# Input projection, token-major rows, merge gates and RWKV-7 in one interleaved stage of a hybrid decoder layer

## What is computed

```python
mod = silu(c) @ w_ada + b_ada                       # sh_m, sc_m, g_m, sh_f, sc_f, g_f
h = x * (1 + sc_m) + sh_m
q_a, kvc, kvs, kvw, g_a, p_b, q_c, k_c, v_c, g_mrg = split(h @ w_in)   # 1024 x 8472
# A: compressed, selected and window attention on q_a, kvc, kvs, kvw, g_a
# B: RWKV-7 on p_b (1792 columns = r, k, v, xw, xa, xg)
prev = concat(shift_prev, p_b[:-1]);  xm = p_b + (prev - p_b) * mu
# per token: decay, a = sigmoid(..), kk = normalised k, then for each of 8 heads
S = S * d + (S @ -kk) (kk * a)^T + v k^T;   out = S @ r
o_b = (groupnorm(out) + bonus) * g
# C: dilated attention, windows (128,1), (512,4), (2048,16), on q_c, k_c, v_c and the caches
m = sum_b sigmoid(g_mrg[b]) * (o_b_branch @ w_br[b])
x = LN(alpha * x + g_m * (m @ w_o));  then a SwiGLU feed-forward and a second LN
```

## Time and profile before

| what | us |
|---|---|
| median of three timed executions | 2869.45 |
| the profiled execution, its own device time | 2877.22 |
| its span, first to last instruction | 2875.4 |
| TensorE busy | 2102.3 (73%) |
| VectorE busy | 1359.8 (47%) |
| ScalarE busy | 297.2 (10%) |
| GpSimd (POOL) busy | 494.6 (17%) |
| granted TensorE clock, mean | 0.81 of full speed |

### The profile page before, as it was taken

One profiled execution on the slowest core, in us unless ns is written; L12 is line 12 of the kernel. 1 busy time (PEld: TensorE's weight loads), 2 busy tenths in 40 slices (PEclk: granted clock), 3 DMA queues, 4 the chain that ended last, 5 costly groups with the idle time before them and its releaser, 6 DMA issues. The chain is left out here.

```text
span 2875.4 us, 36912 instructions
## 1 busy us (share of the span) xinstructions
PE 2102.3 (73%) x15746; PEld 1782.1 (62%) x15746; DVE 1359.8 (47%) x2017; ACT 297.2 (10%) x673; POOL 494.6 (17%) x502
## 2 busy tenths in 40 slices
PE   4999639931346665599994999406785994999995
PEld 2999638810236664599993666303434874999994
DVE  3233202656664444566632566263662336444344
ACT  0111001000200000000002444101211100000000
POOL 0000022110009960222101454202230000000000
PEclk7999869965567555699975698657897997999998
DMA  5433369784013990433303000124354202333220
GB/s 199 155 114 135 106 257 198 196 197 154 0 32 103 322 310 16 148 118 131 112 1 111 1 1 1 36 56 171 129 205 157 69 1 68 88 88 88 81 74 32
DMA packets 229943, 320.40 MB, mean 111 GB/s; under 512 B 91279, under 2 KB 168137, under 8 KB 224596
## 3 DMA queue, kind: packets, MB, share of 16 engines
q1 hardware_dynamic: 184994, 182.63, 20.8%
q0 software_dynamic: 24320, 79.94, 8.6%
q10 hardware_dynamic: 20466, 55.48, 5.7%
HBM read 290.15 MB, written 79.95 MB: 129 GB/s over the span
## 5 line engine op out<-in xcount | busy, mean ns | idle before, releaser
L2344 PE MATMUL sdi_acc<-hT,sdi_w 128*128 128x272 f32 x768 | 178.9, 397 | 15.6 <-DMA sdi_w<-in_w_in_dram 15.6
L1661 POOL TENSOR_SCALAR pat_s<-pat_s,pat_st 128x31 f32<-128x31 f32 (+2 forms) x144 | 127.3, 902 | 287.1 <-DVE pat_st L1689 238.7
L2344 PEld LDWEIGHTS sdi_acc<-hT,sdi_w 128*128 128x128 f32 x768 | 147.6, 192 | 46.9 <-DMA sdi_w<-in_w_in_dram 16.1
L1124 PE MATMUL cmp_pH<-cmp_RTh,cmp_w1h 128*128 128x256 f32 (+1 forms) x576 | 171.2, 297 | 4.9 <-issue 4.9
L269 PE MATMUL ffn_acc<-ffn_hh,ffn_wh 128*128 128x272 f32 x704 | 146.2, 289 | 36.2 <-DVE ffn_wl L260 36.2
L1124 PE MATMUL cmp_pH<-cmp_RTh,cmp_w1l 128*128 128x256 f32 (+1 forms) x576 | 167.8, 291 | 3.0 <-issue 3.0
L1124 PE MATMUL cmp_pH<-cmp_RTl,cmp_w1h 128*128 128x256 f32 (+1 forms) x576 | 167.9, 292 | 0.0
L269 PE MATMUL inp_acc<-inp_hh,inp_wh 128*128 128x272 f32 (+1 forms) x688 | 143.4, 290 | 17.3 <-DVE inp_wl L260 17.3
L269 PE MATMUL ffn_acc<-ffn_hh,ffn_wl 128*128 128x272 f32 x704 | 146.2, 289 | 0.0
L269 PE MATMUL ffn_acc<-ffn_hl,ffn_wh 128*128 128x272 f32 x704 | 145.6, 288 | 0.0
L269 PE MATMUL inp_acc<-inp_hl,inp_wh 128*128 128x272 f32 (+1 forms) x688 | 142.8, 289 | 0.0
(11 more groups left out here) (439 smaller groups left out, 4424.9 us busy)
## 6 DMA issues: line engine op xcount, KB each, us to landing
out_dram<-in_cache_dil_dram SPq DMA_DIRECT2D x1, 32704.0 KB, 155.0
ffn_w<-in_w_ffn_dram SPq DMA_DIRECT2D x60, 512.0 KB, 3.8
sdi_w<-in_w_ada_dram ACTq DMA_DIRECT2D x8, 2048.0 KB
inp_w<-in_w_in_dram SPq DMA_DIRECT2D x7, 2048.0 KB, 7.8
sdi_w<-in_w_in_dram ACTq DMA_DIRECT2D x6, 2048.0 KB
PT<-inp_o ACTq DMA_DIRECT2D x42, 272.0 KB, 2.1
sdi_kv<-in_cache_dil_dram POOLq DMA_DIRECT2D x36, 256.0 KB, 10.0
sdi_kv<-in_cache_dil_dram SPq DMA_DIRECT2D x36, 256.0 KB
```

The source lines that it names most:

```text
L1124: i = pe.matmul(pH[:, w % 2, 0:nw], l, r, start=(q == 0 and n == 0), stop=(q == 15 and n == 2))
L1661: pool.tensor_scalar(s[:, u % 3, b, 0:n], s[:, u % 3, b, 0:n], st[:, u % 4, 2, b:b + 1], None, ALU.mult).then_inc(sd, 1)
L2344: i = pe.matmul(acc[:, n % 2, h, 0:HN], w[:, l % NW, k, j * P:(j + 1) * P], m["hT"][:, k, h * HN:(h + 1) * HN], start=(k == 0), stop=(k == ...
```

## The change

1. `in_projection`, `token_major` and `rwkv` are replaced by one phase, `project_and_mix`, with one block. `Projection` has 67 tiles, now with the 24 gate tiles (so these too are made of three rounded products), in the order p_b, kvc, kvs, kvw, k_c, v_c, g_a, q_a, q_c, gates. A tile's weights come as one load of 512 KB; the cast to the high half is ScalarE's, the subtraction VectorE's. There is one accumulator instead of four. Token-major rows, shift rows and the g_a gates are turned on TensorE from the tile in SBUF (L409, L415), kept by ScalarE, and stored by SP, inside the next tile.
2. `Mixer` does RWKV in 128-token pieces: the 32 sample columns first, then four pieces of the prompt, through elementwise work, chunk pair, state and norm. Several copies out of PSUM (X of every level among them) move from VectorE to ScalarE.
3. Every engine's program is made of Python generators that yield the due time of their next step, in abstract units; `weave` always takes the one that is due first. A piece of the prompt takes 18 units, a projection tile 2.5, and the first 14 tiles (p_b) come before unit 0. So the order on each engine is fixed when the program is built; the waits are the semaphores' as before. The last projection tile is due at unit 132.5; the mixer's last step at about 123.
4. `conditioning` splits h (8 casts on ScalarE, then 8 subtractions on VectorE) at its end, and stores x (8 stores of 272 KB) into rows of PT that are no longer used; `merge` loads it back (8 loads, behind the branch weights and ahead of the gates).
5. `sample_dilated` has no gate tiles any more, only the 8 loads of `w_ada`; softmaxes come after its loads 1, 3 and 5. V is multiplied in its own order instead of through a transposed view. The 81 stores of new cache rows come at the end of its SP program.
6. The four cache copies move from the RWKV chunks' SP program to that of `compress`, behind its first loads.

```diff
+def weave(*programs):
+    heads = [[next(p), i, p] for i, p in enumerate(programs)]
+    while heads:
+        first = min(heads, key=lambda x: (x[0], x[1]))
+        try:
+            first[0] = next(first[2])
+        except StopIteration:
+            heads.remove(first)
...
+    NW = 3
+    ORDER = ("pb", "kvc", "kvs", "kvw", "kc", "vc", "ga", "qa", "qc", "gm")
...
+    def at(self, n, k=0.0):
+        return n - 14 if n < 14 else (n - 14 + k / KD) * PACE
...
+        for n, (c, t, rows) in enumerate(self.tiles):        # Projection.tensor
+            for k in range(KD):
+                yield self.at(n, k)
+                if k == 0:
+                    pe.wait_ge(self.low, n + 1)
+                    if n:
+                        pe.wait_ge(self.evac, n)
...
+ITER = 18
+PROLOGUE = 17
+PACE = 2.5
+def start_of(t):
+    return PROLOGUE + ITER * t
...
 # compress, SP
                 sp.dma_start(per[:, :], a["phi_pe"][0]...).then_inc(loaded, 16)
+                shift_caches(sp, a, m["copied"])
 # merge, SP
+                for k in range(KD):
+                    sp.dma_start(m["xT"][:, k, :], saved_rows(a, k)).then_inc(xl, 16)
                 for n in range(KD):
 # sample_dilated
-SOFTMAX_AFTER = [(2, 3), (5, 3), (9, 3)]
-    loads = [("w_in", c, t) for c, _, t in GROUPS if t >= TILE0["gm"]]
...
-    loads += [("w_ada", k, t) for t in (2 * KD, 4 * KD) for k in range(0, KD, 2)]
+    loads = [(k, t) for t in (2 * KD, 4 * KD) for k in range(0, KD, 2)]
...
+                new_cache_rows(sp, a, m["token_rows_out"])
...
-                    c(dve.tensor_tensor(t3, t3, s[:, g, :].unsqueeze(1).to_broadcast([P, HD, NK]), ALU.mult))
+                    c(dve.tensor_tensor(V[:, :, :], V[:, :, :], s[:, g, :].unsqueeze(2).to_broadcast([P, NK, HD]), ALU.mult))
```

More of the change, by code:

```diff
@@ L50 @@
 TILE0 = {}
+TILES = {}
 GROUPS = []
@@ L210, in _, with saved_rows @@
                 dve.wait_ge(xev, KD)
-                modulate(dve, chain, m["hT"], m["xT"], m["modT"], 0, KD)
+                modulate(dve, chain, hT, xT, m["modT"], 0, KD)
+                dve.sem_inc(modulated, 1)
+                for k in range(KD):
+                    dve.wait_ge(high, k + 1)
+                    split_low(dve, m["hl"][:, k], hT[:, k], m["hh"][:, k]).then_inc(vch, 1)
 ADA_W = 2048
+def saved_rows(a, k):
+    t = TILE0["kvc"] + k if k < TILES["kvc"] else TILE0["vc"] + k - TILES["kvc"]
+    return a["PT"][t * P:(t + 1) * P, :]
 def modulation_step(pe, out, cT, w, k):
@@ L659, with __init__ @@
     HH = HR // 2
[L661 to L670 removed]
+    def __init__(self, nc, a, m, ot, sem, sb):
+        self.a, self.out, self.ot = a, m["sample_state_out"], ot
+        self.S = sb("sS", [P, self.HR, HD])
+        self.tmp = sb("stmp", [P, self.HH, HD])[:, :, :]
+        self.qs = sb("sq_", [P, DT, 5, HD])
+        self.q = [self.qs[:, t] for t in range(DT)]
         self.vs = sb("vs", [P, DT, self.HR])
@@ L875, in _ @@
[L875 to L882 removed]
+                weave(proj.tensor(pe), mix.prepare_tensor(pe), mix.chunk_tensor(pe), mix.state_tensor(pe), mix.norm_tensor(pe))
@@ L1324, in merge @@
         acc = ps("acc", [P, 4, 2, 512])
-        mT = m["hT"]
-        loaded, wol, sig, done, used, ch, out, oused = (sem(s) for s in ("loaded", "wol", "sig", "done", "used", "ch", "out", "oused"))
+        mT = sb("mT", [P, KD, NT])
+        loaded, xl, wol, sig, done, used, ch, out, oused = (sem(s) for s in ("loaded", "xl", "wol", "sig", "done", "used", "ch", "out", "oused"))
         gl = [sem(f"g{i}") for i in range(2)]
@@ L2235, in sample_dilated @@
         wl = [sem(f"w{i}") for i in range(NW)]
-        gdone, gevac, mdone, mevac, mturned, wused = (sem(n) for n in ("gdone", "gevac", "mdone", "mevac", "mturned", "wused"))
-        gst = [sem(f"gst{i}") for i in range(2)]
+        mdone, mevac, mturned, wused = (sem(n) for n in ("mdone", "mevac", "mturned", "wused"))
         NROW = [32, 20, 20]
@@ L2419, in build @@
         with ExitStack() as mixer:
-            for name, chunks in (("hT", KD), ("oaT", 4), ("obT", 4), ("ocT", 2)):
+            m["obT"] = mixer.enter_context(nc.sbuf_tensor("obT", [P, 4, NT], F32))
+            with ExitStack() as first:
+                for name in ("hh", "hl"):
+                    m[name] = first.enter_context(nc.sbuf_tensor(name, [P, KD, NT], F32R))
+                for phase in FIRST:
+                    phase(nc, a, m)
+            for name, chunks in (("oaT", 4), ("ocT", 2)):
                 m[name] = mixer.enter_context(nc.sbuf_tensor(name, [P, chunks, NT], F32))
-            for phase in BEFORE_NSA:
-                phase(nc, a, m)
+            sample_dilated(nc, a, m)
             with ExitStack() as nsa:
+                m["hT"] = nsa.enter_context(nc.sbuf_tensor("hT", [P, KD, NT], F32))
                 m["kcT"] = nsa.enter_context(nc.sbuf_tensor("kcT", [P, DB + 1, 256], F32))
@@ L2443, in _ @@
             sp.wait_ge(m["copied"], 16 * 4)
-BEFORE_NSA = [conditioning, in_projection, token_major, sample_dilated, rwkv]
+FIRST = [conditioning, project_and_mix]
 NSA = [compress, prompt_attention, sample_nsa]
```

1339 lines of the change are left out of this document (733 added, 606 removed).

## The result

Four executions of the changed kernel took 3001.89 to 3017.32 us, median 3013.14; the kernel before 2860.50 to 2870.31, median 2868.39. The ratio is **1.0516, 95% interval 1.049 to 1.0541**: slower by 145 us, where 2812 and faster was forecast, and above the upper end of 2925. The profiled execution took 3001.89 us with a span of 3000.1.

| phase | before | changed | difference | forecast |
|---|---|---|---|---|
| conditioning | 50.8 | 54.6 | +3.8 | +8 |
| projection, token-major rows, RWKV | 783.4 | 803.7 | +20.3 | −28 |
| dilated attention | 324.2 | 299.3 | −24.9 | −62 |
| compress | 357.8 | 482.3 | **+124.5** | +20 |
| prompt and sample attention | 682.3 | 679.5 | −2.8 | 0 |

What follows compares the result with a forecast made beforehand. It took TensorE to bound the projection and nothing full to bound RWKV, whose gaps projection matmuls would fill. Terms: conditioning +8, stage −28, dilated attention −62, compress +20, merge +5, together −57, giving 2812 us; range 2700 to 2925.

Steps and rivals of the forecast that it cites:

- Compress: Compress phase: copies start with the gathers, which run at half of 316 GB/s; only first fill and small loads exposed, +20 us.
- Rival 1: Compress: copies starve the gathers by alternating packet by packet, so compress loses 135 us instead of 20; total 2927; chance 0.22.
- Stage: Merged projection and RWKV phase: 755 us (650 to 870), replacing 783, so −28.
- VectorE against POOL: Stage: VectorE operations with two SBUF inputs slowed beside POOL, 69 us on VectorE, of which half shows: 35 (0 to 110).
- Evacuation: Stage: with one accumulator a tile waits for ScalarE's copy, about 0.9 us at 55 of 66 transitions: 50 (40 to 90).
- SP's queue: Stage: weight loads and stores stand behind the 82 loads of the samples' operands: 14 us (0 to 31).
- TensorE's work: Stage: 402 us for 67 projection tiles, 130 for RWKV's 64x64 products, 50 for lora, head sums and turns.
- Round trips: Stage: RWKV's exposed TensorE gaps, 94 us before, half hidden by projection matmuls: 45 us (0 to 94).
- Dilated attention: Dilated attention phase: without gate tiles, 39 MB at 193 to 200 GB/s plus the ending, 262 us instead of 324: −62.
- Conditioning: End of conditioning: eight ScalarE casts and eight VectorE subtractions added, +8 us (6 to 11).
- Rivals 2 and 3: Stage: engines wait for each other, stage 920, total 2977, chance 0.08; TensorE's clock at 0.80, +100, total 2912, chance 0.09.
- Rival 4: Better: round trips and port absorbed by TensorE's work (−70), dilated stage down to 245; total 2725; chance 0.16.

Runs made afterwards that it cites:

- e7: Changed kernel with the cache copies, still in compress, cut into 4 to 4.7 KB pieces ordered so that no two neighbours touch; ratio 1.0071 to the kernel before.
- e1: Changed kernel with the four cache copies issued at the end of SP's program in the prompt attention instead of compress; ratio 1.0025 to the kernel before.
- e4: Changed kernel without the samples' recurrence on POOL, so their state and RWKV output are not computed; ratio 1.0278 to the kernel before.
- e5: e1 with the 82 loads of the samples' operands moved from SP's queue to POOL's; ratio 0.9958 to the kernel before.
- e6: e5 with the 81 stores of new cache rows moved from the dilated attention to compress, behind its first loads; ratio 0.9921 to the kernel before.
- e12: Kernel before with only the V multiply of the dilated attention put in V's own order; ratio 0.9964 to the kernel before.
- e11: e9 plus the accumulator taken out in two halves of 272 columns; ratio 0.9685 to the kernel before.
- e9: e6 with POOL's recurrence started after the last prompt piece's elementwise part, its stores on POOL's queue, the samples' norm behind the last tile; ratio 0.9842.
- e3: Changed kernel with the cache copies' rows, still in compress, cut into pieces of 4 to 4.7 KB that touch; ratio 1.0497 to the kernel before.

## Why the prediction was wrong, step by step

**Compress (+20, was +124.5).** This is the step that failed, and it turned the sign. The prediction priced the copies beside the gathers "at half of 316": it shared bandwidth by bytes. Rival 1 had the mechanism, the place, the packet sizes (57 and 3.6 KB) and nearly the price (135), and got 0.22. The reason given against it was that in 378 to 406 a queue of 2.0 KB packets was not pushed aside by one of 3.3 KB. That row does not speak against alternation by packets: with sizes so near, alternation gives near shares too. Nor was it a test: a third queue, SP's, had 18.5% in the same window, and all three together filled 76% of the engines' time, so nothing shows that the two compared were both full.

```profile
q1 hardware_dynamic: 1186, 1.93, 18.5%
```

A row in which both theories say the same was taken for one that decides. What the runs put in its place: packets 639 to 639, 545 to 543, 647 to 648 and 1631 to 1628 where both queues were full, and with like packets (e7) a loss of 9 us against e1. The Trainium skill, page DMA: Bandwidth & Descriptors, section Queues, rings and completion order, states this rule, that an engine serves the queues in turn and changes only between packets; the counts above agree with it to 1%.

**Stage (755, was 803.7).** It was inside its own bounds, 49 over. TensorE's busy time and its list of waits divide that: 29 are work that wasn't in the sum and 20 waits for VectorE; SP's queue has 4 more, evacuation 6 less. By terms:

- *VectorE against POOL*: 35, measured 61.6 (e4). That VectorE is held up beside POOL was right, and so was the price on VectorE: 69 estimated, 77.5 more busy time measured. What failed is "half shows": four fifths of it reached the stage, 57 of the 61.6 as waits of TensorE for VectorE. The longest of them, in TensorE's timeline, ended right behind the fourteen operations of L810 shown above, which stood ahead of its answer. The Trainium skill, page SBUF — State Buffer, section SBUF: two separate sides, has whichever of the two instructions starts first hold the shared ports for its whole length; single operations of up to 2.498 us beside POOL's of 2.34 agree with it. The upper price of 170 us on VectorE that the prediction worked out with it was not reached.

```profile
298.51 1.13 PE L875 MATMUL rw_B<-rw_bb,rw_kkf 64*64 64x64 f32 x32 [22.08 <-DVEq L935]
```

- *Evacuation*: 50; TensorE waited 44.1 in 56 waits. A lone tile took 1.18 more than with four accumulators (7.18 less 6.0), but only the 0.79 of it that was read from the earlier trace rows is the wait; the other 0.39 is in TensorE's busy time.
- *SP's queue*: 14; the stall was 18.2 us, and e5 gained 8 in the profile, 19 in the median. Right within that.
- *TensorE's work*: 582 and 15 more for the clock, while the records show 626 us busy between 58 and 858, and 622 without POOL (e4). The short term is the projection tiles: by the windows for their accumulator they cover 481.7 us, 7.2 a tile, where 67 by 6.0 were taken from tiles that ran alone on four accumulators. The rest has at least 144, where 180 was forecast. A record of a tile can overlap those of RWKV's matmuls beside it, so part of the 80 is theirs; how much isn't shown.

```profile
54.60:858.30 803.70, 481.72 (x3216) 432.19 (x3216) 41.81 (x67) 0.90 0.30 82
```

- *Round trips*: 45; TensorE's waits for VectorE without POOL are 42.7 (e4). Right.

**Dilated attention (−62, was −25).** The V multiply was right to 0.01 us, and the waits for softmaxes are gone (1.7 us in all). Two terms failed, and one of them by luck cost nothing in the sum. First, the stores at the end of SP's program "cost nothing": they ended the phase, 14.4 us behind VectorE's last instruction, and e6 got 19 us back. Their issue, 66 us for 81, was longer than the 42 us of VectorE's work that was named as cover; the two numbers weren't set against each other. But the sum also had 15 us "of ending" behind VectorE, and the stores just filled these. Second, and this is most of the 37 missing, the transfers: "39 MB at 193 to 200 GB/s" were 42.5 MB at 183, 232 us instead of 200. The 4 MB of RWKV's load that I took off are issued at the very end of that window and lay mostly beyond it, and the rate belonged to a mixture with the gates' large loads.

**What held.** Conditioning (+3.8 for +8) and merge (0 for +5) were small. The move of the copies out of the chunks gave 6 us there at most, and the prediction had none. With the copies put right, the change is at 1.0025 and not at 0.98: of the 57 us forecast, 49 were lost in the stage and 37 in the dilated attention; some 27 came back from conditioning (4), merge (5) and compress (18: it took 339.3 us in e1 and 337.4 in e12, where 20 more were forecast).

**Rivals.** Rival 1 happened. Rivals 2 and 3 didn't: the stage was 804 and not 920, the clock 0.96 in the lone tiles and 0.94 from 450 to 740. Only from 230 to 450, with TensorE busy 57% of the time, was the clock 0.78, and e4 has it at 0.89 there. Rival 4 had the stage at 685; e11, after repairs, has it at 716.8.

## What to carry to other kernels

Before a bulk copy is moved to a phase that "has room", compare packet sizes, not bandwidths: a queue of small packets beside one of large packets gets its share by count, and the latency of the first small transfer becomes the length of the bulk copy. Put such a copy where nothing is waited for (here the prompt attention, at no cost), or cut it so that pieces don't touch.

When work is woven into small pieces, count instructions and not elements where another engine holds them up (a piece of 0.35 us took 1.38 here), and ask of each queue whether its issue time is longer than the cover named for it; an effect of either kind is repaired by moving one instruction stream (e5, e6, e9), and the weave then pays: 0.9685.

A row speaks against a rival only if the rival says something else of that row than the forecast does.

## What the runs showed of the hardware that was not expected

- Two queues that were both full had equal numbers of packets, though of unlike size: 639 of 59 KB and 639 of 3.7 KB, 1631 of 4.0 KB and 1628 of 3.6 KB. A DRAM-to-DRAM copy whose pieces touch had packets of 57 to 59 KB even when its access pattern was cut into 4 KB pieces (e3); only pieces that don't touch kept 4.4 KB (e7). With the scattered pieces SP needed 48.9 us to issue three copies; with the touching ones of e3 1.88, as with the uncut rows:

```profile
1168.09 48.87 SPq L547 DMA_DIRECT2D out_dram<-in_cache_dil_dram  x3
```

- A copy of 128x272 on ScalarE out of PSUM takes 0.397 us and one of 128x544 0.624, so a half costs 64% of the whole.
- A VectorE instruction of 128x128 that takes at most 0.353 us without POOL's recurrence (e4) took up to 2.498 beside it. TensorE's waits for VectorE in one and the same stage were 103.7 us in one profile (e5) and 84.9 in another (e6); that this comes from how many of the instructions meet POOL's is likely, but not shown.
